# The last block of a two-layer feed-forward: plain products by halves of the tokens instead of Strassen's sums, and the side input turned inside that block

## The reference, cut to what matters

```
h = h + concat([pool_out, attn_out]) @ w_out[i]
hn = rmsnorm(h, norm2[i])
h = h + square(relu(hn @ w_up[i])) @ w_down[i]          # 1024 -> 4096 -> 1024
gate = sigmoid(rmsnorm(h, norm3[i]) @ w_gate[i])
h = h + gate * (p[i] @ w_ple[i])                        # p[i]: 1024 tokens x 256
```

## Time and profile before

| | us |
|---|---|
| median of 3 runs (3279.0, 3280.49, 3283.15) | 3280.49 |
| the profiled execution | 3277.44 |
| its span, first to last instruction | 3275.7 |
| PE busy | 3177.0 (97%) |
| DVE busy | 2076.2 (63%) |
| POOL busy | 1730.0 (53%) |
| ACT busy | 1021.1 (31%) |

### The profile page before, as it was taken

How to read it: one execution, slowest core, us unless ns; L and a number is a source line. 1 busy time by engine, 2 the same in 40 slices (tenths; PEclk the granted TensorE clock), 3 DMA queues, 4 the chain that set the end, 5 groups by cost and what they waited for, 6 DMA issues and landing times.

```text
span 3275.7 us, 39576 instructions
## 1 busy us (share of the span) xinstructions
PE 3177.0 (97%) x14732; PEld 2499.9 (76%) x14732; DVE 2076.2 (63%) x2815; ACT 1021.1 (31%) x1903; POOL 1730.0 (53%) x1566
## 2 busy tenths in 40 slices
PE   7999999999999899999999999999899999899997
PEld 6776788888888687767788888887687666688886
DVE  6546476666666855554676666666755988797223
ACT  3223253333333421232343333333421344302112
POOL 5523356666666546432466666666444533376574
PEclk9999999999999999999999999999999999999999
DMA  5111211111111221112131111111111100011112
GB/s 156 40 42 32 83 58 52 52 52 52 54 52 52 61 86 54 38 40 83 39 60 52 52 52 52 54 52 52 51 39 52 33 20 27 20 49 46 49 58 78
DMA packets 306351, 173.75 MB, mean 53 GB/s; under 512 B 61424, under 2 KB 296944, under 8 KB 306160
## 3 DMA queue, kind: packets, MB, share of 16 engines
q1 hardware_dynamic: 285824, 162.49, 17.2%
q10 hardware_dynamic: 20336, 8.73, 0.9%
HBM read 155.13 MB, written 12.91 MB: 51 GB/s over the span
## 4 chain that ended last, share of the span: by engine, by line
PE 86%; DVE 10%; issue 2%; ACT 1%; DMA 0%; DVEq 0%; ACTq 0%; SPq 0%
PE ring L1203 17%; PE ring L1205 16%; PE ring L1204 16%; PE aux L1203 4%; PE aux L1205 4%; PE aux L1204 4%; PE ring L1437 4%; PE ring L1439 3%; PE ring L1438 3%; PE aux L1437 2%; PE aux L1439 2%; PE aux L1438 2%; DVE left L2536 2%; PE aux L1297 1%; PE aux L1273 1%
## 5 line engine op out<-in xcount | busy, mean ns | idle before, releaser
L951 POOL TENSOR_TENSOR w_hi<-w_raw,ones 128x512 fp32r<-128x512 f32 (+3 forms) x392 | 430.4, 1098 | 885.3 <-PE ring L1205 723.6
L1203 PE MATMUL ring<-Q_hi,w_hi 128*128 128x512 f32 x1328 | 529.3, 399 | 2.9 <-DVE s_half L2558 1.7
L954 POOL TENSOR_TENSOR w_lo<-w_raw,w_hi 128x512 fp32r<-128x512 f32 (+3 forms) x392 | 509.6, 1300 | 30.7
L1204 PE MATMUL ring<-Q_lo,w_hi 128*128 128x512 f32 x1328 | 519.4, 391 | 0.0
L1205 PE MATMUL ring<-Q_hi,w_lo 128*128 128x512 f32 x1328 | 519.2, 391 | 0.0
L1203 PE MATMUL ring<-P_hi,w_hi 128*128 128x512 f32 x768 | 322.2, 420 | 9.5 <-DVE pool_u L2149 5.3
L1203 PEld LDWEIGHTS ring<-Q_hi,w_hi 128*128 128x128 f32 x1328 | 250.7, 189 | 80.9 <-issue 30.5
L1205 PE MATMUL ring<-P_hi,w_lo 128*128 128x512 f32 x768 | 301.9, 393 | 0.0
L1204 PE MATMUL ring<-P_lo,w_hi 128*128 128x512 f32 x768 | 301.3, 392 | 0.0
L1205 PEld LDWEIGHTS ring<-Q_hi,w_lo 128*128 128x128 f32 x1328 | 250.7, 189 | 53.4
L1204 PEld LDWEIGHTS ring<-Q_lo,w_hi 128*128 128x128 f32 x1328 | 250.9, 189 | 50.6 <-issue 1.0
(11 more groups left out here) (364 smaller groups left out, 6970.5 us busy)
## 6 DMA issues: line engine op xcount, KB each, us to landing
w_raw<-in_w_in SPq DMA_DIRECT2D x84, 512.0 KB, 3.8
w_raw<-in_w_up SPq DMA_DIRECT2D x64, 512.0 KB, 4.0
w_raw<-in_w_down SPq DMA_DIRECT2D x64, 512.0 KB, 3.4
h_scratch<-h ACTq DMA_DIRECT2D x16, 512.0 KB, 3.2
w_raw<-in_w_gate SPq DMA_DIRECT2D x16, 512.0 KB, 3.9
hx<-h_scratch SPq DMA_DIRECT2D x12, 512.0 KB, 6.5
x_raw<-in_x SPq DMA_DIRECT2D x8, 512.0 KB, 7.8
w_raw<-in_w_out SPq DMA_DIRECT2D x16, 256.0 KB, 2.9
```

Of the source, the lines that this page charges most:

```text
L951: g.tensor_tensor(w_hi[:, slot, ks], w_raw[:, slot, ks], one.broadcast_to([P, width, P]), ALU.mult).then_inc(w_hi_ready, 1)
L954: g.tensor_tensor(w_lo[:, slot, ks], w_raw[:, slot, ks], w_hi[:, slot, ks].bitcast(F32), ALU.subtract).then_inc(w_ready, 1)
L1203: t.matmul(o, wh, xh, start=first, stop=False)
L1204: t.matmul(o, wh, xl, start=False, stop=False)
```

## The change

The last of the eight blocks of each layer does its down panels plainly: `plain_pair`, four products of twelve matmuls for each of the four panels, in the order chunk 0 hf 0, chunk 1 hf 0, chunk 0 hf 1, chunk 1 hf 1 (`PLAIN`). Its weights are split as every other panel's are. Its hidden values are only squared and split (`raise_last`, `take_last`), its products only added to `h` (`add_plain`). `h` is prepared for the gate in the order of these products, each one behind the add of the next. All four `turn_p` stand in the last block's up panels 1 and 3, and the loads and low parts of p move with them: `load_p` hf 0 goes to the block's first panel, hf 1 to its third, `lower_p` ahead of the split of its panels 3 and 5. The numbers of the semaphores' steps follow.

```diff
+def late_at(r, hf):
+    return 2 * FFN - 0.2 + 0.01 * (2 * r + hf)
+LAST = BLOCKS - 1
+PLAIN = [(0, 0), (1, 0), (0, 1), (1, 1)]
-HN3_WITHIN = {0: [], 1: HN3_ORDER[0:2], 2: HN3_ORDER[2:5], 3: HN3_ORDER[5:8]}
-HN3_AFTER = HN3_ORDER[8:9]
-HN3_BETWEEN = {("turn_p", 0, 0): HN3_ORDER[9:10], ("turn_p", 1, 0): HN3_ORDER[10:16]}
+HN3_ORDER = [(2 * j + e, hf) for j in range(UP) for e, hf in PLAIN]
...
-            put(GATE_AT + 2 * hf, (0, 3, 1, 4)[2 * hf + c], "turn_p", c, hf)
+            put(late_at(1 + 2 * hf, c), 2, "turn_p", c, hf)
...
@@ SP @@
-                if n == GATE:
-                    load_ple(l, 1)
-                    sp.wait_ge(side_done, side_no(l, "turn_p", 1, 0) + 1)
-                    load_p(l, 1)
-                if n == GATE - 1:
-                    sp.wait_ge(prod_done, prods_before(l, GATE - 2))
-                    load_p(l, 0)
+                if n == GATE - 2 * UP:
+                    sp.wait_ge(prod_done, prods_before(l, GATE - 2 * UP - 2))
+                    load_p(l, 0)
+                if n == GATE - 2 * UP + 2:
+                    sp.wait_ge(side_done, side_no(l, "turn_p", 1, 0) + 1)
+                    load_p(l, 1)
...
@@ POOL @@
-                if n == GATE + 1:
+                if n in (GATE - 2 * UP + 3, GATE - 2 * UP + 5):
                     for c in range(2):
-                        lower_p(l, c, 0)
+                        lower_p(l, c, (n - GATE + 2 * UP) // 2 - 1)
...
@@ PE @@
+        def plain_pair(l, j):
+            ...
+            for k, (e, hf) in enumerate(PLAIN):
+                to = use_starts(l, ffn_use(LAST, r, k))
+                for i in range(UP):
+                    if k == 0 and i % 2 == 0:
+                        pe.wait_ge(w_ready, 2 * g + 1 + i // 2)
+                    if j == 0 and e == 0:
+                        pe.wait_ge(hid_ready, last_hid_no(HID_LOWS, l, i, hf) + 1)
+                    x, cols = last_hid(i, hf), slice(e * P, e * P + P)
+                    mm = triple(to, hi[:, i, cols], lo[:, i, cols], hid_hi[x][:, i % 2], hid_lo[x][:, i % 2], i == 0, i == UP - 1)
+                mm.then_inc(prod_done, 1)
...
@@ ACT @@
+        def raise_last(l, r, hf):
+            y = y_hid(l, LAST, r, hf)
+            act.wait_ge(drained, drain_no(l, LAST, r, hf) + 1)
+            square_starts(y)
+            a.activation(squares[y % 2], tmp[:], ACT.Square).then_inc(squared, 1)
+            act.wait_ge(squared, y + 1)
+            a.activation(hid_hi[last_hid(r, hf)][:, r % 2], squares[y % 2], ACT.Copy).then_inc(hid_high, 1)
...
+            for r in range(UP):
+                for hf in range(2):
+                    woven(l, late_at(r, hf))
+                    raise_last(l, r, hf)
+            raise_h(l, HN3_ORDER)
...
@@ DVE @@
+        def take_last(l, r, hf):
+            ...
+            v.scalar_tensor_tensor(tmp[:], ffn_banks[ffn_use(LAST, r, hf) % 5], 0.0, rstd[:, half_cols(hf)], ALU.max, ALU.mult).then_inc(drained, 1)
+            dve.wait_ge(hid_high, last_hid_no(HID_HIGHS, l, r, hf) + 1)
+            v.tensor_tensor(hid_lo[x][:, r % 2], squares[y % 2], hid_hi[x][:, r % 2].bitcast(F32), ALU.subtract).then_inc(hid_ready, 1)
+        def add_plain(l, i):
+            ...
+            v.tensor_tensor(at, at, ffn_banks[ffn_use(LAST, r, k) % 5], ALU.add).then_inc(drained, 1)
...
+            for i in range(4 * UP):
+                add_plain(l, i)
+                if i:
+                    lower_h(l, HN3_ORDER[i - 1:i])
+            lower_h(l, HN3_ORDER[-1:])
```

More of the change, by code:

```diff
@@ L675, in h_no @@
     def h_no(l, b, j, k):
-        return 3 * (UP * (BLOCKS * l + b) + j) + (C22, C12, C21).index(k)
+        return 3 * (UP * (LAST * l + b) + j) + (C22, C12, C21).index(k)
     def pair_ended(engine, l, f, hf):
[L681 to L685, removed]
+        engine.wait_ge(drained, drain_no(l, LAST, UP + f // 2, PLAIN.index((f % 2, hf))) + 1)
     def half_cols(hf):
@@ L690, in is_pair @@
     def is_pair(g):
-        return g < ALL and FFN <= g % PANELS < GATE and (g % PANELS - FFN) % (2 * UP) >= UP
+        return g < ALL and FFN <= g % PANELS < GATE - 2 * UP and (g % PANELS - FFN) % (2 * UP) >= UP
     def pair_no(g):
@@ L1465, in _ @@
                 for r in range(UP):
-                    for hf in up_order(r):
+                    for hf in up_order(b, r):
                         half_up(l, b, r, hf)
                 for j in range(UP):
-                    pair_down(l, b, j)
+                    if b == LAST:
+                        plain_pair(l, j)
+                    else:
+                        pair_down(l, b, j)
             for f in range(KC):
@@ L1678, in square_starts @@
                 r, second = divmod(i, 2)
-                if r < 2:
+                if b == LAST:
+                    act.wait_ge(hid_ready, last_hid_no(HID_LOWS, l, r, second) + 1)
+                elif r < 2:
                     act.wait_ge(hid_sum, hid_no(HID_SUMS, l, b, T1, r) + 1)
@@ L1904, in _ @@
                     upper(Q_hi, gains[:, l, 1], f, hf)
-            for b in range(BLOCKS):
+            for b in range(LAST):
                 for r in range(UP):
@@ L1909, in _ @@
                             high_weights(l, b, 0, part)
-                    for s, hf in enumerate(up_order(r)):
+                    for s, hf in enumerate(up_order(b, r)):
                         if b == 0 and r == 0:
@@ L2315, in take_hidden, with add_pair @@
                 lower_of(T4, low(T4))
-        def add_pair(l, b, j, within):
+        def take_last(l, r, hf):
+            y, x = y_hid(l, LAST, r, hf), last_hid(r, hf)
+            dve.wait_ge(prod_done, prod_no(l, LAST, r, hf) + 1)
+            dve.wait_ge(squared, y)
+            if r == 0 and hf == 0:
+                dve.wait_ge(drained, drain_no(l, LAST, 0, 0))
+            v.scalar_tensor_tensor(tmp[:], ffn_banks[ffn_use(LAST, r, hf) % 5], 0.0, rstd[:, half_cols(hf)], ALU.max, ALU.mult).then_inc(drained, 1)
+            dve.wait_ge(hid_high, last_hid_no(HID_HIGHS, l, r, hf) + 1)
+            v.tensor_tensor(hid_lo[x][:, r % 2], squares[y % 2], hid_hi[x][:, r % 2].bitcast(F32), ALU.subtract).then_inc(hid_ready, 1)
+        def add_plain(l, i):
+            (f, hf), (j, k) = HN3_ORDER[i], divmod(i, 4)
+            r, at = UP + j, h[:, f, half_cols(hf)]
+            dve.wait_ge(prod_done, prod_no(l, LAST, r, k) + 1)
+            if f % 2 == 0 and hf == 0:
+                dve.wait_ge(drained, drain_no(l, LAST - 1, r, C11) + 1)
+            else:
+                dve.wait_ge(h_added, h_no(l, LAST - 1, j, ((C11, C12), (C21, C22))[f % 2][hf]) + 1)
+            v.tensor_tensor(at, at, ffn_banks[ffn_use(LAST, r, k) % 5], ALU.add).then_inc(drained, 1)
+        def add_pair(l, b, j):
             r, c0, c1 = UP + j, half_cols(0), half_cols(1)
@@ L2432, in _ @@
                 for j in range(UP):
-                    add_pair(l, b, j, HN3_WITHIN[j] if b == BLOCKS - 1 else [])
-            lower_h(l, HN3_AFTER)
+                    add_pair(l, b, j)
+            for r in range(UP):
+                for hf in range(2):
+                    take_last(l, r, hf)
+            for i in range(4 * UP):
[3 more added lines that the diff above has]
+            lower_h(l, HN3_ORDER[-1:])
             for f in range(KC):
```

67 lines of the change are left out of this document (34 added, 33 removed).

## The result

The median is 3248.41 us (3246.16 to 3249.74, 4 runs) against 3279.74 us (3278.98 to 3283.15, 4 runs): 31.3 us less, ratio 0.9899, 95% interval 0.9885 to 0.9914. The forecast was 3247 us, range 3243 to 3256. The profiled execution after has a span of 3246.9 us, 28.8 us shorter.

What follows compares the result with a forecast made beforehand. PE, busy nearly all of the span, was taken as the bound. Gains of 16.7 and 16.8 us in the two layers (33.5 us) gave a span of 3242.2, an execution of 3243.9 and, with 3.05 us added, 3247 us; range 3243 to 3256.

Steps and rivals of the forecast that it cites:

- The frame: Whole kernel: PE is busy nearly all of the span; an added matmul costs 0.2266 us and nothing covers it.
- The removed losses: Layer 0: 5.45 us lost in the down panels and 16.71 us in the gate's first panel all go.
- What stays: Four `turn_p` and two `stat3` still cost PE 3.52 us a layer, in the gate or in the up panels.
- DVE in the plain panels: Last block's down panels: DVE needs 2.15 us a product against PE's 2.72, 34 us in 43.5, so no wait.
- Rival B: Plain panels: POOL holds up low parts of `h`, DVE is late at T; 3250.4, up to 3257 us; chance 0.10.
- The head of the gate: Gate's first panel: operands of `h` come in time, first gate product taken at T + 11.3, only PE bounds.
- The margins: Time to spare before PE waits: 2.9 us at the hidden values, 9.5 us at the banks.
- C: Rival: one ring of waits stays at another place, say 5 us a layer; 3257 us; chance 0.05.
- D: Rival: DVE bounds the plain panels at the bank wait, a loss beyond 3.77 us a product; 3294 us; chance 0.03.
- E: Rival: late `h`, not the place of `turn_p`, holds the gate, so its waits stay; 3280.5 us; chance 0.02.
- the 7.00 us wait: Gate: PE stands before the fourth `turn_p` because ACT's copy for the third stands behind the gate's first half.
- With no gap the clock has no cause to fall: Last block to gate: granted clock stays 1.00, as in all stretches without such gaps.

Runs made afterwards that it cites:

- more_matmuls: The changed kernel with the first of the four plain products of each panel made twice (96 matmuls more in all): 3271.16 us.
- by_chunks: The changed kernel with each panel's four plain products ordered by chunks of output features instead of by halves of the tokens: 3248.29 us.
- dve_plus2: The changed kernel with two more DVE instructions of about 0.69 us each ahead of each plain add: 3268.84 us.
- p_in_gate: The changed kernel with all work on p put back at its old places at the gate, the last block still plain: 3258.33 us.

## Why the prediction was right

Point by point, by its own steps. T is the end of the last plain product.

**The frame** (PE full, so time is won where PE stands still and every matmul costs) held: 0.2267 us a matmul in more_matmuls for the 0.2266 used.

**The removed losses.** 5.45 and 16.71 us a layer were to go in full, and did: no wait of PE is left between the last block and the gate's second panel in either layer. Which half of the change removes which wait did not enter the sum, since it takes all of them away at once.

**What stays.** Four `turn_p` and two `stat3` were put at 3.52 us. The two `stat3` are 15.40 - 13.60 = 1.80 us, forecast 1.76; the four `turn_p` 1.96, forecast 1.76. The sum was 33.5 us and the stretches gave 33.1; this is nearly all of the difference.

**DVE in the plain panels.** Forecast 34 us in the panels, measured 35.05; right for a wrong reason. From the first add to the last low part DVE worked 38.2 us, 4.5 us of it behind T. The low part was taken at its median of 0.78 us and was 1.21 in the mean: eight of the sixteen in layer 0 took 1.70 to 1.86 us. Rival B's premise was true for half of them, and the rule of the Trainium skill ("SBUF — State Buffer", "Who interferes with whom"), that a VectorE instruction with two SBUF inputs contends with a GpSimd instruction that reads SBUF, agrees with this trace. The change had put them beside POOL's splits. But DVE still idled 8.5 of the 43.52 us, and the low part that the gate's first product needs last, chunk 7 of hf 0, met no split on POOL and ended at T - 0.57 us (forecast T - 0.6), so it cost PE nothing. The additions to the sum of squares and the adds were at their rows.

**The head of the gate.** The first gate product was to be taken at T + 11.3; it was at 1116.30 - 1105.69 = 10.6 us. The margins held: hidden values (by_chunks took 2.7 us of theirs away and lost nothing), DVE (one more instruction a product, nothing).

**The rivals.** C: none of the rings stayed. D: dve_plus2 shows its size and corrects its place. There the plain adds stand 3.61 us apart (1070.40 to 1117.33 us for thirteen), still below the 3.77 us at which the prediction set break-even, and 20 of the 31 us were gone; D's own sum would be 16 x (3.61 - 2.72) = 14.2 us a layer, more than the 9.2 and 9.5 measured. And PE's loss came at the gate's low part, not at the bank's wait in the plain panels. E was refuted, and yet its idea had a share. The prediction put the 7.00 us wait to the place of p's copy alone; p_in_gate shows that with `h` early, half of it goes although p's copies stand where they were. The sum did not depend on it, as both parts are in the change.

**Luck.** The median came within 1.4 us of the forecast (3248.4 for 3247) although the span missed by 4.7 us (3246.9 for 3242.2). The forecast added 3.05 us because the median before lay that much above its profiled execution; after, the median lay 0.2 us below it. Nothing in the prediction gave a reason for that difference.

**What was not foreseen** are, in the profiled executions, the 2.9 us in the third layer and 1.5 us near 60 us. "With no gap the clock has no cause to fall" was true of the changed stretches; the gaps of other stages were taken as fixed in price, and they are not.

## What to carry to other kernels

Where a stage trades PE's work against sums on other engines, and its neighbours wait for those engines, count both: here 24 matmuls more a layer cost 5.4 us, the waits that they removed inside the stage were worth just that, and the gain came wholly from the stage behind. Small jobs that share one PSUM bank form a ring through another engine's list; put them where that engine has time and where nothing in its list stands ahead that waits for PE. And when a change moves later stages in time, expect short waits elsewhere to change in price by a clock level and back: compare stretch by stretch before a shortfall is blamed on the change.

## What the runs showed of the hardware

The same third layer, with the same instructions, took 805.7 to 806.9 us in eight profiles and 808.2 to 808.7 us in four, whose marks lie within 2.1 us of each other. Later by 3.0 and 5.6 us, 300 us of it were granted a clock of 0.99 and 1.00 instead of 0.97. A wait of 1.97 us was followed by the low level (1.2 GHz) in one profile and by nothing in another. What decides between the two is open.

A VectorE low part (both large inputs in SBUF) took 0.73 to 0.75 us in all 54 cases of the changed kernel's trace in which GpSimd stood idle at its start. In all 53 in which one of GpSimd's weight splits (`w_hi` or `w_lo`) was running at its start it ended 0.55 us behind the end of that split, whenever it had begun, and so took 0.81 to 1.87 us. The last five, which met other GpSimd work (`ple_lo` and small ones), took 0.73 to 0.74 us. A VectorE operation with one input in PSUM (the plain add, the addition to `sumsq`) kept to 0.67 to 0.69 us throughout.
